# Half groups of early products spread over the short steps of a hybrid decoder kernel, `sk` skewed by head, and the page maximum read first

## The reference

```python
h = RMSNorm(x); z = h @ w_in            # one projection for all branches and gates
# A: gated DeltaNet, 4 heads, chunks of 128 here: conv, SiLU, L2-norm of q and k, decay,
#    triangular solve, S = g*S + k^T v
# B: latent attention, 8 heads: low-rank q, 128-wide latent, rotary key; prompt causal,
#    samples against 2048 past rows fetched by page_table
# C: mLSTM, 4 heads: C = decay*C + w*k^T v, running-max stabiliser
x += (sigmoid(g_a)*(o_a@w_a) + sigmoid(g_b)*(o_b@w_b) + sigmoid(g_c)*(o_c@w_c)) @ w_out
x += down(silu(causal_dwconv3(gate) + bias) * up)      # after a second RMSNorm
```

## Time and profile before

| | |
|---|---|
| median of 3 runs | 1306.99 us (1306.63 to 1307.66) |
| the profiled execution | 1302.87 us |
| its span, first to last instruction | 1300.7 us |
| mean granted clock of TensorE | 0.992 |
| TensorE busy | 1278.8 us, 98% |
| VectorE, ScalarE, GpSimd busy | 544.2, 253.4, 153.5 us |
| early and other weight products (L546) | 75% of the chain that ended last |

### The profile page before, as it was taken

The page is one execution under the profiler, slowest core; times in us unless marked ns, Lnnn a source line. Parts: engine busy times, 40 slices in busy tenths (PEclk is TensorE's granted clock), DMA queues, the critical chain, the costliest instruction groups (busy, mean ns, idle before and its releaser), DMA issues.

```text
span 1300.7 us, 18321 instructions
## 1 busy us (share of the span) xinstructions
PE 1278.8 (98%) x7326; PEld 1047.6 (81%) x7326; DVE 544.2 (42%) x1360; ACT 253.4 (19%) x640; POOL 153.5 (12%) x210
## 2 busy tenths in 40 slices
PE   7999999999999999999999999999999999999997
PEld 6878777768888888888888787786788888888885
DVE  7874745231135333321277836533311353333212
ACT  3432424221000111110034232341210001111000
POOL 2012441200000000010001125402000000000000
PEclk9999999999999999999999999999999999999999
DMA  9423475613454444464444235645134444444440
GB/s 338 158 84 100 131 253 200 226 50 99 146 151 146 146 146 146 148 219 152 148 156 136 89 99 191 218 164 205 59 114 146 151 146 146 146 147 150 155 138 34
DMA packets 59604, 194.32 MB, mean 149 GB/s; under 512 B 7824, under 2 KB 8112, under 8 KB 56704
## 3 DMA queue, kind: packets, MB, share of 16 engines
q1 hardware_dynamic: 50544, 152.22, 36.2%
q0 software_dynamic: 8768, 40.84, 8.8%
q10 hardware_dynamic: 208, 0.09, 0.0%
HBM read 183.86 MB, written 9.25 MB: 148 GB/s over the span
## 4 chain that ended last, share of the span: by engine, by line
PE 95%; DVE 4%; issue 1%; ACT 1%; DMA 0%; SPq 0%; DVEq 0%; ACTq 0%
PE banks L546 75%; PE banks L1005 2%; PE banks L1012 1%; PE banks L911 1%; PE banks L1051 1%; PE banks L1015 1%; PE banks L669 1%; PE banks L629 1%; PE banks L822 1%; PE banks L923 1%; DVE arena L1627 1%; PE banks L938 1%; PE banks L790 0%; PE banks L954 0%; DMA arena<-in_x 0%
## 5 line engine op out<-in xcount | busy, mean ns | idle before, releaser
L546 PE MATMUL banks<-arena 128*128 128x264 f32 x4544 | 1035.4, 387 | 7.4 <-DVE arena L1522 6.7
L546 PEld LDWEIGHTS banks<-arena 128*128 128x128 f32 x4544 | 856.4, 190 | 167.3 <-issue 10.8
L1140 ACT ACTIVATE arena<-banks 128x256 f32<-128x256 f32 (+10 forms) x252 | 95.9, 404 | 416.7 <-PE banks L546 281.9
L2108 DVE TENSOR_SCALAR arena<-arena 128x256 f32<-128x256 f32 x44 | 18.2, 414 | 130.3 <-ACT arena L1140 130.0
L2141 DVE SCALAR_TENSOR_TENSOR arena<-banks,arena 128x264 f32<-128x264 f32 x16 | 6.9, 433 | 135.3 <-PE banks L546 135.3
L2318 POOL COPY arena<-arena 128x2 f32<-128x2 f32 x44 | 13.7, 311 | 377.6 <-ACT arena L1140 275.9
L1171 ACT ACTIVATE arena<-banks 128x264 f32<-128x264 f32 x32 | 12.6, 392 | 126.1 <-PE banks L546 126.1
L1714 DVE SCALAR_TENSOR_TENSOR arena<-arena,banks 128x264 f32<-128x264 f32 x16 | 6.9, 430 | 65.7 <-PE banks L546 65.7
L1005 PEld LDWEIGHTS banks<-arena 128*128 128x128 f32 x256 | 29.1, 146 | 6.0 <-issue 6.0
L1005 PE MATMUL banks<-arena 128*128 128x128 f32 x256 | 32.4, 281 | 0.0
L1448 ACT ACTIVATE arena<-arena 128x256 f32<-128x256 f32 x44 | 18.4, 418 | 66.4 <-DVE arena L2110 66.3
(11 more groups left out here) (429 smaller groups left out, 1085.6 us busy)
## 6 DMA issues: line engine op xcount, KB each, us to landing
arena<-in_weights SPq DMA_DIRECT2D x230, 512.0 KB, 3.5
arena<-in_weights SPq DMA_DIRECT2D x112, 256.0 KB, 3.0
arena<-in_s POOLq DMA_DIRECT2D x2, 2048.0 KB, 12.1
out_ss_o<-arena POOLq DMA_DIRECT2D x16, 256.0 KB, 3.0
arena<-in_mla_w POOLq DMA_DIRECT2D x4, 1024.0 KB, 7.3
arena<-in_c POOLq DMA_DIRECT2D x4, 512.0 KB, 5.9
out_sc_o<-arena POOLq DMA_DIRECT2D x16, 128.0 KB, 3.5
arena<-in_x SPq DMA_DIRECT2D x4, 264.0 KB, 5.0
```

Of the source, the lines that this page charges most:

```text
L546: mm = nc.tensor.matmul(dst, ring[:, at_:at_ + 128], rhs[:, j, :], start=(start and j == 0), stop=(stop and j == k - 1))
L1140: return A(dst, src, ACT.Copy, scale=scale)
L2108: link(ts(cv, fc[:, j % 3, 0:TP], w[0], par[:, Q_FB + j:Q_FB + j + 1], ALU.mult, ALU.add))
```

## The change

Four edits, the same in both layers, with the calls of `half` on ScalarE and VectorE changed to match:

1. A half group after `bcL` 4 to 7 and one after `bcB`; one after `bcM` and one after `bcI`.
2. `half(4)` after `mc1` becomes `half(2)`, with one half after the first four `out` and one after the last four. With 1, the run at the end of the paged stage falls from 24 to 20 half groups; the places between hold the same number of halves as before, with products that stand four further on in `EARLY` (six between `bcI` and `out`).
3. `sk`: in step m head h takes sample n = (m + h) % 8 instead of n = m.
4. In VectorE's `top`, the maximum is reduced before the halves' evacuations, not after.

```diff
@@ TensorE
                 for i in range(4, 8):
                     lengths(i)
+                half(1)
                 for h in range(NH):
                     spread("bcB", h, R_B)
+                half(1)
                 for i in range(4):
                     lengths(i)
...
                 for h in range(NH):
                     spread("bcM", h, R_M, 0, TP)
+                half(1)
                 for h in range(NH):
                     spread("bcI", h, R_INT, P - NB, TT)
+                half(1)
...
-                for n in range(NB):
+                for m in range(NB):
                     for h in range(NH):
+                        n = (m + h) % NB
                         mm = nc.tensor.matmul(b[32 * h:32 * h + 32, 0:P], windows[:, h, 32 * n:32 * n + 32], S[:, h * NB + n, :],
-                                              start=(n == 0), stop=(n == NB - 1), skip_group_check=True)
+                                              start=(m == 0), stop=(m == NB - 1), skip_group_check=True)
...
-                half(4)
+                half(2)
...
                 for j in range(4):
                     outer(j)
+                half(1)
                 pe.wait_ge(*at(l, "oa_squares", 1))
...
                 for j in range(4, 8):
                     outer(j)
+                half(1)
@@ ScalarE
                 A(l2row, bank("l2")[:, 0:TT], ACT.Sqrt, scale=l2_scale, bias=l2_bias).then_inc(*read("l2"))
-                half(2)
+                half(4)
...
                 act.wait_ge(*evac(l, "s2"))
+                half(2)
...
-                half(4)
+                half(2)
                 act.wait_ge(*evac(l, "os"))
...
+                half(1)
                 act.wait_ge(*out(l, "na"))
                 A(nrow, bank("na")[:, 0:TT], ACT.Sqrt, scale=n_scale, bias=n_bias).then_inc(*read("na"))
+                half(1)
@@ VectorE
-                half(3)
+                half(5)
                 dve.wait_ge(*at(l, "conv_state", 1))
...
-                half(5)
+                half(6)
                 dve.wait_ge(*at(l, "s_decayed", 8))
...
                 last.then_inc(*read("mc2"))
-                half(3)
+                half(4)
...
-                def top(g):
+                def top(g, n):
                     dve.wait_ge(*out(l, "ss", g))
                     link(V.tensor_reduce(rmax[:, g:g + 1], bank("ss", g), AX_X, ALU.max))
                     dve.wait_ge(*evac(l, "sn"))
                     tt_(rmax[0:32, g:g + 1], rmax[0:32, g:g + 1], snew[:, g:g + 1], ALU.max).then_inc(*up("page_max"))
+                    half(n)
                     dve.wait_ge(*out(l, "mxT", g))
...
-                half(1)
-                top(0)
+                top(0, 1)
...
-                half(2)
-                top(1)
+                top(1, 2)
```

More of the change, by code:

```diff
@@ L115, in schedule @@
     add("l2"); half(2)
-    add("bcL", 4, "V", 4); add("bcB", 4, "V"); add("bcL", 4, "V")
+    add("bcL", 4, "V", 4); half(1); add("bcB", 4, "V"); half(1); add("bcL", 4, "V")
     add("kT", 2); add("aq", 8, "V"); half(1)
@@ L128, in schedule @@
     add("vn0"); half(1); add("s1"); add("o0"); add("ks", 1, "V"); half(1); add("vn1"); half(1); add("o1"); add("s2", 1, "V")
-    add("bcM", 4, "V"); add("bcI", 4, "V")
+    add("bcM", 4, "V"); half(1); add("bcI", 4, "V"); half(1)
     add("mkT", 2); add("mvT", 2); add("sk", 1, "V"); add("mqk", 2, "V"); add("os", 1, "V"); half(1)
-    add("mn0"); add("mc1"); half(4)
-    add("out", 4, "V"); add("na"); add("out", 4, "V", 4)
+    add("mn0"); add("mc1"); half(2)
+    add("out", 4, "V"); half(1); add("na"); add("out", 4, "V", 4); half(1)
     add("mn1"); add("mc2", 1, "V"); half(3)
```

## The result

The kernel after takes 1293.56 us (median of 4 runs, 1293.43 to 1293.71); the kernel before, run beside it, 1307.12 us (4 runs, 1306.63 to 1307.66). The ratio is 0.9896, with 0.9879 to 0.9913 as its 95% interval: 1.0% faster. The prediction was 1294.3 us, in 1288.5 to 1300.5.

What follows compares the result with a forecast made beforehand. TensorE, busy 98% of the span, bounds it, so only lost time counts: narrow spreads, `top(0)` idle, half clock. Layer 0's 5.04 plus layer 1's 7.70 give 12.7 us: 1290.2 profiled, plus 4.1 makes 1294.3 us, range 1288.5 to 1300.5.

Steps and rivals of the forecast that it cites:

- the likeliest case: Whole kernel: the forecast of 1294.3 us, with its own 1291 to 1297, chance 0.56.
- (a): Halves before and after `bcB`, at the length and beta spreads: waits filled, gain 1.43 us a layer, between 0.83 and 2.2.
- (b): Halves after `bcM` and `bcI`: gain 2.41 us in layer 0, 3.37 in layer 1, with a new 1.4 us wait at `mn0`.
- (d): `half(4)` after `mc1` split 2 + 1 + 1: -0.3 us a layer, between -0.6 and 0; `out` a tie, wait up to 0.5.
- The clock term of (a): Half-clock stretch in `aq` of layer 1, at the length spreads: it goes, gaining 1.7 us once.
- more clock comes back: Rival: half-clock stretches of other executions, as at layer 0's lengths or the small matmuls, vanish too: 1290.9 us, chance 0.17.
- The stretch after `sn`: Half clock at 883.31 after very small matmuls in layer 1: named a candidate to differ by execution, not in the sum.
- (c): `sk` skewed by head: slow because of half clock, not a tile conflict; priced at nothing, between 0 and 1.3 us a layer.
- (e): Page maximum reduced before the half in VectorE's `top(0)`: TensorE's 1.40 us idle goes, gain 1.5 us a layer.
- Half the gain: Rival: fills come late in the queue that counts, `out` waits 0.5, no clock back: 1300.2 us, chance 0.20.
- no effect: Rival: waits only shift from the spreads to `mn0` and `out`; time stays within 0.2%, chance 0.04.
- slower: Rival: new waits and narrow groups between halves each bring half clock of 1.7 us: 1311 us, chance 0.03.

Runs made afterwards that it cites:

- e6: Changed kernel with one more half group before `mn0`, taken from the end of the paged stage: 1290.76 us, ratio 0.9872 to the kernel before.
- e1: The kernel before, unedited, run and profiled once more: 1309.37 us, ratio 1.0012.
- e7: Changed kernel with one half group in the middle of `sn`, taken from the end of the paged stage: 1293.49 us, ratio 0.9893 to the kernel before.
- e11: Changed kernel with one more half before `mn0` and the four halves after `mc1` in one run: 1289.89 us, ratio 0.9875 to the kernel before.
- e2: Changed kernel with `sk` in its old unskewed order (n = m): 1293.52 us, ratio 0.9885 to the kernel before.
- e4: Kernel before with only the halves before and after `bcB` added: 1297.33 us, ratio 0.9920.
- e5: Kernel before with only the halves after `bcM` and after `bcI` added: 1300.64 us, ratio 0.9951.
- e8: Changed kernel with both one more half before `mn0` and one in the middle of `sn`: 1290.77 us, ratio 0.9871 to the kernel before.
- e12: Changed kernel with GpSimd's gathers of pages 4 to 7 held until VectorE read the second page's last transpose: 1292.51 us, ratio 0.9904 to the kernel before.
- e10: Changed kernel with VectorE's `top` in its old order, maximum after the halves' evacuations: 1292.23 us, ratio 0.9895 to the kernel before.

## Why the prediction was right, and where its steps were not

**The total.** 1294.3 forecast, 1293.56 measured, and the likeliest case was the one that came. But the sum was carried by two errors of opposite sign: the profiled pair lost 9.4 us where 12.7 were forecast, and the 4.1 us between the profile and the median of before, which I kept for after, were gone (after: 1293.43 profiled, 1293.56 median). The first made the forecast 12.7 - 9.4 = 3.3 us too low, the second 4.1 - 0.1 = 4.0 too high.

**The waits** were sized well, from equal shapes elsewhere in the trace. The spreads of (a): 5.94 forecast, 5.93 measured. (b): `bcM` to `mkT` 4.93 forecast, 4.96 measured; from `bcM` to `mn0` 13.33 forecast, 147.52 - 133.98 = 13.54 measured, with 1.22 of waiting for 1.4. The chain ScalarE, GpSimd, VectorE was indeed what came late next, and e6 takes it away by giving TensorE work for its length. (d): -0.3 forecast, -0.28 measured; `out` did not wait. The end of the stage had no cover to lose: 20 halves run on without a wait, and the distance from `cmb` to `ov` is 7.14 us shorter in layer 0 and 7.13 in layer 1, four times 1.78.

**The clock term of (a)** is the step that was mis-sized. I took 1.7 us, once, because the first profile had one stretch of 3.42 us there, and gave layer 0 as much only "if that one had it in other executions", outside the sum. e1 has it in both layers at 6.82 us: 3.4 us each. The rival "more clock comes back" named the right mechanism and the right place. Most of it was taken back by what follows. What I called against it, that nothing shows the other executions, was an absence of evidence: the gap between profile and median was a sign of it, and I should have moved it to the places that the edits touch. The prediction also puts operands of two or four rows before all four slow stretches; before the fourth stand matmuls of one column.

**The stretch after `sn`** offset it. I listed it as a candidate that the change leaves alone. In the pair of traces it appeared in layer 0 (1.7 us lost), and in layer 1 it stayed. Had it gone, the stall behind it would have taken the gain, as in e7. One of the four runs of after shows the same: 1293.46 us at clock 0.998, beside 1293.43 at 0.995. In e11, without a stall, the same difference in clock is worth 3.4 us.

The Trainium skill, TensorE: Matmul & The Clock Gate, "What's actually happening", has activity release the throttle and its absence bring it back. The traces agree in two kinds of place: at the end of the span, where TensorE's work runs out (after: the last matmul starts at 1282.9, half clock from 1284.7), and in layer 1 of e2, after the idle 1.97 us. Idle times of 1.9 to 2.6 us in e4, e5, e7 and e8 were followed by no half clock. The other 27 stretches of the 14 traces follow spreads of two or four rows or matmuls of one column, with TensorE busy throughout (e1: PE 6.82 of 6.82 us in the window at 79.32), and none is left where the spreads are filled with full-width work (after, e2, e6 to e12). That narrow operands bring it fits these places and is not shown by more than them; why one execution has a stretch and another not stays open.

**The stall at the second page** was not foreseen. It cost 0.48 us in layer 0 and 0.70 in layer 1 of after: from the second page's transposes to the third's it is 6.04 us (254.08 to 260.12) and 6.26, against 5.56 from the third to the fourth. It costs more where the clock is full (e7: 7.53 from the first page's to the second's).

**(c)** held: `sk` was slow by the clock alone (e2).

**(e)** had the right 1.5 us, and the right instruction in the way, but the wrong edit behind it. The prediction said that the `wa` halves that stood there "are earlier now", and still put the gain down to VectorE's order. e10 has the old order and no wait.

**Half the gain, no effect, slower.** None came. The 1.22 us idle at `mn0` was followed by no half clock, nor were the narrow groups between halves. The mechanism of the slower case did not act in this pair; e2 shows one stretch of its kind.

## What to carry to other kernels

Where narrow matmuls stand one behind the other and their readers set the pace, put full-width work between them: it hides the readers' time, and here it also ended half-clock stretches that cost more than the waits (e4 gained 10.5 us, of which 2.9 are waits). When one profile lies well below the median of the runs, ask which places in it can differ by execution before you carry the difference over. After each gain read which wait comes last next: one half more before `mn0` gave 2.8 us, and the clock won after `sn` gave nothing while a stall lay behind it. Before an edit is credited with ending a stall, look whether the unedited kernel has executions without it: here the kernel before has both.

## What the runs showed of the hardware

- One program's executions differed by 6.5 us (1305.20 to 1311.70), and the mean granted clock with them (0.992 to 0.985). The half-clock windows last 3.4 or 6.8 us, at the same few places.
- `sk`, with four groups of columns reading tiles 4 KB apart, runs at 273 ns a matmul, with or without the skew.
- Beside a burst of eight indirect gathers the semaphore updates of TensorE's transposes came late, and ScalarE and VectorE with them by up to 3.6 us (e4: 4.27 in place of 0.70), in 7 of the 12 traces that have the gathers early; in two more the readers of the page before were late and TensorE idled. The other three have no stall.
- The nine traces with a stall lack part of the gathers' own semaphore updates (115 to 133 of 256 on record), the five without one lack none. The cause is open.
